# Second attention of a two-layer decoder trunk: both heads of a pair in one job for maxima and shifts, one score bank per head, weight sums on GpSimd alone

## The reference

```python
def mla_attention(h, w_in, q_norm, kv_norm, w_uq, w_ukv, w_o):
    ...                                   # q: 16 heads x (64 + 32), k: 64 + shared 32, v: 64
    def attend_block(args):               # one block of 128 queries, all 16 heads
        qn, qp, b = args
        q_pos = N_META + b * BLOCK + jnp.arange(BLOCK)
        s = (jnp.einsum('bqhd,bshd->bhqs', qn, k_nope)
             + jnp.einsum('bqhd,bsd->bhqs', qp, k_pe)).astype(jnp.float32)
        s = jnp.where(k_pos[None, :] <= q_pos[:, None], s, NEG_INF)
        p = jax.nn.softmax(s, axis=-1).astype(v.dtype)
        return jnp.einsum('bhqs,bshd->bqhd', p, v)
    ...
    return o @ w_o
```

## Time and profile before

| | |
|---|---|
| median of 3 executions | 3991.29 us (3990.94 to 4009.18) |
| profiled execution | 3988.05 us, of it 3986.3 us from the first to the last instruction |
| TensorE busy, whole span | 3469.2 us, 87% |
| VectorE, GpSimd, ScalarE busy | 2007.0, 1575.1, 1245.8 us |
| mean granted TensorE clock | 0.927 |
| second attention | about 1772 to 3024 us of the span |

### The profile page before, as it was taken

One profiled execution on the slowest core, in us unless ns is written; L12 is line 12 of the kernel. 1 busy time (PEld: TensorE's weight loads), 2 busy tenths in 40 slices (PEclk: granted clock), 3 DMA queues, 4 the chain that ended last, 5 costly groups with the idle time before them and its releaser, 6 DMA issues. The chain is left out here.

```text
span 3986.3 us, 60756 instructions
## 1 busy us (share of the span) xinstructions
PE 3469.2 (87%) x20523; PEld 2575.8 (65%) x20524; DVE 2007.0 (50%) x4183; ACT 1245.8 (31%) x2374; POOL 1575.1 (40%) x1257
## 2 busy tenths in 40 slices
PE   7999997996999959969999999999997996999920
PEld 5777775785888859955555555555554885888810
DVE  3555444674333336635666666666553653333306
ACT  3444444221222224432233233233223221222201
POOL 2222221343444315435665655655542223444302
PEclk8999998997999979977999999999898997999965
DMA  2101103554988849960101101101004447988519
GB/s 89 35 24 35 35 24 95 159 153 164 353 299 307 290 154 252 267 166 6 45 9 48 45 9 45 34 20 48 6 9 131 148 135 253 330 301 306 201 56 335
DMA packets 370814, 540.15 MB, mean 136 GB/s; under 512 B 94879, under 2 KB 291535, under 8 KB 363328
## 3 DMA queue, kind: packets, MB, share of 16 engines
q1 hardware_dynamic: 343584, 461.28, 37.0%
q0 software_dynamic: 27040, 76.40, 4.9%
HBM read 399.22 MB, written 146.96 MB: 137 GB/s over the span
## 5 line engine op out<-in xcount | busy, mean ns | idle before, releaser
L1965 POOL TENSOR_TENSOR ab_acc<-ab_acc,ab_pT 128x1024 f32<-128x1024 f32 (+4 forms) x208 | 424.4, 2040 | 491.4 <-ACT ab_pT L2009 486.7
L2009 ACT ACTIVATE ab_pT<-ab_S 128x1024 f32<-128x1024 f32 (+2 forms) x360 | 321.9, 894 | 864.3 <-PE ab_S L2110 536.5
L2021 DVE TENSOR_REDUCE ab_mx<-ab_W 128x1 f32<-128x400 f32 (+4 forms) x720 | 377.2, 560 | 374.8 <-PE ab_W L2124 207.4
L2167 PE MATMUL ab_O<-ab_pT,ab_v 128*64 128x512 f32 (+4 forms) x1408 | 353.7, 581 | 0.0
L2108 PE MATMUL ab_S<-ab_q_hi,ab_k_hi 97*128 97x512 f32 (+2 forms) x720 | 319.0, 443 | 0.9 <-DVE ab_q_hi L2038 0.9
L2124 PE MATMUL ab_W<-ab_k_hi,ab_q_hi 96*128 96x400 f32 (+4 forms) x720 | 246.9, 401 | 83.6 <-DMA ab_maskT<-in_mask_bT 28.5
L2108 PEld LDWEIGHTS ab_S<-ab_q_hi,ab_k_hi 97*128 97x128 f32 x720 | 142.1, 197 | 270.4 <-ACT ab_pT L2009 133.0
L1324 PE MATMUL ex_G<-ex_xT,ex_wg 128*128 128x160 f32 x2048 | 295.4, 303 | 5.2 <-DMA ex_wu<-in_moe_w_up 5.2
L1324 PEld LDWEIGHTS ex_G<-ex_xT,ex_wg 128*128 128x128 f32 x2048 | 284.6, 193 | 9.5 <-DMA ex_wu<-in_moe_w_up 6.0
L1324 PE MATMUL ex_U<-ex_xT,ex_wu 128*128 128x160 f32 x2048 | 288.6, 299 | 0.0
L1324 PEld LDWEIGHTS ex_U<-ex_xT,ex_wu 128*128 128x128 f32 x2048 | 281.6, 190 | 0.0
(11 more groups left out here) (297 smaller groups left out, 7195.9 us busy)
## 6 DMA issues: line engine op xcount, KB each, us to landing
ex_wg<-in_moe_w_gate SPq DMA_DIRECT2D x64, 1024.0 KB, 5.8
ex_wu<-in_moe_w_up SPq DMA_DIRECT2D x64, 1024.0 KB, 9.8
ex_wd<-in_moe_w_down SPq DMA_DIRECT2D x64, 1024.0 KB, 12.5
pr_o<-scratch_oT SPq DMA_DIRECT2D x34, 512.0 KB, 4.8
scratch_h<-pr_h SPq DMA_DIRECT2D x34, 512.0 KB, 4.9
scratch_xn<-pr_xn SPq DMA_DIRECT2D x34, 512.0 KB, 2.7
pb_y<-scratch_y SPq DMA_DIRECT2D x17, 1024.0 KB, 8.2
fi_y<-scratch_y SPq DMA_DIRECT2D x16, 1024.0 KB, 8.7
```

The lines of the kernel that those rows point to most:

```text
L1965: nc.gpsimd.tensor_tensor(to, to, pT[0:r, U % RING, :, 0:n], ALU.add).then_inc(added_pool, 1)
L2009: nc.scalar.activation(pT[0:r, U % RING, :, 0:n], S[0:r, U % 2, :, 0:n], ACT.Exp, scale=B_SCALE).then_inc(exped, 1)
L2021: nc.vector.reduce_max(mx[:, h, t, c:c + 1], W[:, j % 2, 0:n], AX.X).then_inc(emptied, 1)
L2167: last = nc.tensor.matmul(O[HD * h:HD * h + HD, G % 2, 512 - n:512], v[0:r, p % 2, h, b, :], pT[0:r, U % RING, h, 0:n], start=(U == opens[ ...
```

## The change

**Jobs of two heads.** `W` becomes four banks: two slots of two banks, one bank for each head. A scan or shift job now covers both heads, so there are half as many, and each is one instruction on VectorE over both banks (`W[:, j % 2, :, 0:n]`). On TensorE the two heads' scans come first and their two masks behind. The limits that fill `work[U]` are halved with the count.

**One score bank per head.** `S` becomes two banks. The scores of head h in unit U wait until the exponential of head h in unit U - 1 has read them (`exped`, counted per head now). ScalarE does one exponential per head instead of one over both: 720 instead of 360.

**Sums on GpSimd alone.** `on_dve`, `acc2` and the merging add are gone; GpSimd does all 352 sums.

**Six probability buffers** instead of four (`RING`), and a buffer `den0` of its own for tile 0. SyncE issues the four constants ahead of the first pair's loads instead of behind them.

The core of the diff:

```diff
-    RING = 4
+    RING = 6
-    def on_dve(U):
-        p, g, b = units[U]
-        return 0 < g < NG and b > 0 and (U - opens[p, g]) % 5 in (1, 3)
...
-        while taken < len(scans) and taken < (12 if U < 0 else min(2 * U + 44, 4 * U + 18)):
+        while taken < len(scans) and taken < (6 if U < 0 else min(U + 22, 2 * U + 9)):
...
-        S = s.ps("S", [P, 2, 2, 512])
+        S = s.ps("S", [P, 2, 512])
         O = s.ps("O", [P, 2, 512])
-        W = s.ps("W", [P, 2, 512])
+        W = s.ps("W", [P, 2, 2, 512])
...
-                load(0)
-                sp.dma_start(ident[:, :], io["ident"]).then_inc(consts, 16)
                 sp.dma_start(identb[:, :], io["identb"]).then_inc(consts, 16)
                 sp.dma_start(mask[:, :], io["mask_b"]).then_inc(consts, 16)
+                sp.dma_start(ident[:, :], io["ident"]).then_inc(consts, 16)
                 sp.dma_start(maskT[:, :], io["mask_bT"]).then_inc(consts, 16)
+                load(0)
...
-                    if U == closes[p, g]:
-                        if g > 0:
-                            pool.wait_ge(added_dve, dve_adds[U])
-                            nc.gpsimd.tensor_tensor(acc[:, G, :, :], acc[:, G, :, :], acc2[:, G, :, :], ALU.add).then_inc(merged, 1)
...
-                    nc.scalar.activation(pT[0:r, U % RING, :, 0:n], S[0:r, U % 2, :, 0:n], ACT.Exp, scale=B_SCALE).then_inc(exped, 1)
+                    for h in range(2):
+                        act.wait_ge(scored, 2 * U + h + 1)
+                        nc.scalar.activation(pT[0:r, U % RING, h, 0:n], S[0:r, h, 0:n], ACT.Exp, scale=B_SCALE).then_inc(exped, 1)
...
-                    nc.vector.reduce_max(mx[:, h, t, c:c + 1], W[:, j % 2, 0:n], AX.X).then_inc(emptied, 1)
+                    nc.vector.reduce_max(mx[:, :, t, c:c + 1].rearrange("p h a -> p (h a)"), W[:, j % 2, :, 0:n], AX.X).then_inc(emptied, 1)
...
-                    if 1 <= U <= NU and on_dve(U - 1):
-                        add(U - 1)
...
-                    if U >= 2:
-                        pe.wait_ge(exped, U - 1)
                     for h in range(2):
-                        to, qs = S[:, U % 2, h, 0:n], slice(at, at + n)
+                        to, qs = S[:, h, 0:n], slice(at, at + n)
+                        if U >= 1:
+                            pe.wait_ge(exped, 2 * U + h - 1)
...
-                    pe.wait_ge(merged, G + 1)
+                    pe.wait_ge(added, adds[closes[p, g]])
```

More of the change, by code:

```diff
@@ L1801, in attention_b @@
             for t in ([0] if g == 0 else []) + list(tiles_of(g)):
-                scans += [(p, g, h, t, c) for c in range(len(chunks_of(t))) for h in range(2)]
+                scans += [(p, g, t, c) for c in range(len(chunks_of(t)))]
     work = {U: [] for U in range(-1, NU + 8)}
@@ L1814, in attention_b @@
                 if g == 0:
-                    at.append(("shift", p, NG, 0))
-                at += [("shift", p, g, h) for h in range(2)]
+                    at.append(("shift", p, NG))
+                at.append(("shift", p, g))
                 assert U < 0 or U + 1 < opens[p, g]
@@ L1829, in attention_b @@
     pv_counts = [pv_count(U) for U in range(NU)]
-    dve_adds = [sum(1 for V in range(U + 1) if on_dve(V)) for U in range(NU)]
-    pool_adds = [sum(1 for V in range(U + 1) if units[V][1] < NG and not on_dve(V)) for U in range(NU)]
+    adds = pv_counts
     with ExitStack() as ctx:
@@ L1978, in _ @@
                     p, u = divmod(U, PU)
-                    if units[U][1] < NG and not on_dve(U):
+                    if units[U][1] < NG:
                         add(U)
@@ L2111, in score @@
                         if diagonal:
-                            last = nc.tensor.matmul(S[:, U % 2, h, 0:P], identb[:, :], maskT[:, :], start=False, stop=True)
-                    last.then_inc(scored, 1)
+                            last = nc.tensor.matmul(S[:, h, 0:P], identb[:, :], maskT[:, :], start=False, stop=True)
+                        last.then_inc(scored, 1)
                 def room(j):
@@ L2117, in room, with scan @@
                         pe.wait_ge(emptied, j - 1)
[L2119 removed]
+                def scan(j, p, g, t, c):
                     lo, n = chunks_of(t)[c]
@@ L2123, in scan, with shift @@
                     diagonal = c == len(chunks_of(t)) - 1
[L2124 to L2125 removed]
+                    for h in range(2):
+                        last = nc.tensor.matmul(W[:, j % 2, h, 0:n], q_hi[0:QD, p % 2, h, P * t:P * t + P], k_hi[0:QD, p % 2, h, lo:lo + n],
+                                                start=True, stop=not diagonal)
                     if diagonal:
                         d = min(P, n)
[L2128 removed]
+                        for h in range(2):
+                            last = nc.tensor.matmul(W[:, j % 2, h, n - d:n], identb[:, :], mask[:, 0:d], start=False, stop=True)
                     last.then_inc(filled, 1)
[L2131 removed]
+                def shift(j, p, g):
                     pe.wait_ge(m_ready, NG * p + g % NG + 1)
                     room(j)
[L2134 to L2136 removed]
+                    for h in range(2):
+                        for k in range(1 if g == NG else 4):
+                            one = m[:, h, 0:1] if g == NG else m[:, h, 4 * g + 1 + k:4 * g + 2 + k]
+                            last = nc.tensor.transpose(W[:, j % 2, h, P * k:P * k + P], one.to_broadcast([P, P]), ident[:, :])
                     last.then_inc(filled, 1)
@@ L2140, in divide @@
                     G = NG * p + g
-                    pe.wait_ge(merged, G + 1)
+                    pe.wait_ge(added, adds[closes[p, g]])
                     room(j)
                     for h in range(2):
-                        last = nc.tensor.matmul(W[HD * h:HD * h + HD, j % 2, :], ones[:, :], acc[:, G % 2, h, :], start=True, stop=True)
+                        last = nc.tensor.matmul(W[HD * h:HD * h + HD, j % 2, 0, :], ones[:, :], acc[:, G % 2, h, :], start=True, stop=True)
                     last.then_inc(filled, 1)
@@ L2153, in early @@
                         weights = pT[0:META, U % RING, h, 0:P]
-                        nc.tensor.matmul(W[HD * h:HD * h + HD, j % 2, 0:P], v[0:META, p % 2, h, 0, :], weights, start=True, stop=True)
-                        last = nc.tensor.matmul(W[HD * h:HD * h + HD, j % 2, P:2 * P], ones[0:META, :], weights, start=True, stop=True)
+                        nc.tensor.matmul(W[HD * h:HD * h + HD, j % 2, 0, 0:P], v[0:META, p % 2, h, 0, :], weights, start=True, stop=True)
+                        last = nc.tensor.matmul(W[HD * h:HD * h + HD, j % 2, 0, P:2 * P], ones[0:META, :], weights, start=True, stop=True)
                     last.then_inc(filled, 1)
```

70 lines of the change are left out of this document (18 added, 52 removed).

## The result

The changed kernel takes 3828.76 us, the median of four executions (3818.64 to 3833.54), against 3991.11 us for the kernel before beside it (3977.01 to 4009.18): ratio 0.9587, 95% interval 0.9544 to 0.9631. In the profiled executions it is 3818.64 us against 3988.05, 169 us less. The forecast was 84 us less. A later run of the same changed kernel gave 3831.64 us and a ratio of 0.9558 (0.9517 to 0.9599).

The account below looks back on a forecast made before the run. TensorE was taken to set the pace, stopped by waits on `W` for VectorE. Waits 65 us, merge 2.4, masks 5 and clock 12 sum to 84 us: 3904 us profiled, forecast 3907 us, range 3850 to 3969.

Parts of the forecast that it names:

- The rows of the waits: TensorE's five listed waits on `W` for VectorE: 73.6 us in 133 waits go, 20 us (10 to 35) stay.
- The uncounted part: Time lost at TensorE's waits on `W` beyond the listed waits: 23 us at most, nothing at least, 11 taken.
- half of seven such dips: Clock falls at the starts of pairs of heads, 3.4 us each; half of seven go, 12 us won (-20 to 60).
- Rival 1: TensorE gets full clock from the stage's start, where 61 us at half level cost 30: 3877 us; chance 0.12.
- Masks, constants, merge: In the stage: masks behind both scans win 5 us (0 to 14), constants first 0, the end merge's removal 2.4.
- The cover: GpSimd falls 3 us behind in group 3 and may fall 12 before the divide waits: no cost.
- the worked-out 899: GpSimd's busy time in the stage with all sums on it, 899 us, up from 712.
- Rival 3: GpSimd becomes the bound with full sums at 3.11 us, 159 us a pair against 153.5: 4004 us; chance 0.04.
- rival 2: ScalarE's two exponentials, 0.171 us longer per unit than one, hold TensorE: 62 us more, 3969 us; chance 0.06.
- Rivals 4 and 5: More of the stage at half clock: 250 us more gives 4032 us, 130 to 205 gives 3972 to 4010; 0.05 each.

Follow-up runs that it names:

- the split alone: The kernel before with only one score bank and one exponential per head changed: 4078.1 us, ratio 1.0188 (1.0146 to 1.0229).

## Why the prediction was right in sign and half in size

**What bounds, and what goes.** Right. TensorE set the pace, its stops were on `W`, and the room on `W` removed them: 160 of 170 us hang on it.

**The rows of the waits.** 78.6 less 15.1 is 63.5 us won; the forecast was 53.6, from five rows of 73.6 with 20 staying. Five us were missed because the small rows were left out of the sum, and five because 15 stay and not 20. Right within its bounds. What stays behind the shifts is 1.1 us a pair where 1.3 was worked out.

**The uncounted part: the first term that failed.** I put 11 us on it, half of 133 x 0.17, "because some of the spacing is there without a wait too". After, 95 to 103 us are won without the clock. Less 63.5 for the rows and 7 for the masks, 24 to 33 remain over the 126 stops that went, which is 0.19 to 0.26 us each. This is worked out as a remainder and not measured alone, but it holds in a single clean pair as well: 149.78 - 135.13 = 14.7, less 1.4 for the clock, 9.0 for rows (10.4 in 18 waits before, 1.4 in 2 after) and 0.9 for masks, leaves 3.4 over 16 stops, 0.2 each. So the whole of the 0.12 to 0.23 us by which a modelled end lies too late came back at each stop, and halving it was the error. That none of this spacing is there without a wait is an inference from the sizes; no run tests it.

**The clock: the step that failed most.** "I let half of seven such dips go: 12 us." It was about 53 to 62, of up to 75. Three things were missed. All dips went, not half. The long half-level stretches in pairs 4 and 7 were taken as chance, though the one in pair 4 begins right behind a stop of 1.19 us; together these pairs lost up to 27 us. And the half-level stretch at the stage's start ended at 1793 us instead of 1837, where I took it as given because TensorE was busy 55.9 of 61 us. That gave up to 21 us. The changed kernel's second run rose only near 1807 us, so a part of this is chance, but not all: in the ten traces of kernels with more room on `W` it rose between 1792 and 1810 us and stayed up through the first pair. In the two kernels with two banks for `W` and four for the scores it rose at 1837 and 1841. In the two with two banks for each it rose near 1810, but fell again to half for 31 us twice. Rival 1, which got 0.12, named the recovery at the start but not its size elsewhere. By the rule of the Trainium skill ("TensorE: Matmul & The Clock Gate", section "Why this matters for your kernels"), to keep TensorE busy without gaps, 63 us more had been worked out beside it, 3844 us in all. The measured time is 3828.76 us. The later pairs of the trace agree with it; the first, busy 158 of 166 us and at 0.92, does not fully. I weighed one row against the rule, the dense stretch at half clock, though such a stretch only shows that density does not lift the clock at once, not that stops do not lower it.

**Masks, constants, merge.** 7 us for 5, 0 for 0, 2.6 for 2.4: right.

**The sum.** Of the 169.4 us, rows are 63.5, the uncounted part 24 to 33, masks 7, the clock 53 to 62, the merge 2.6 and the earlier start, by chance, 4.3; the last 6 stay open.

**Sums on GpSimd.** The cover held: 855.0 us busy in the stage where 880 to 920 were expected. Of the 44 us under the worked-out 899, shorter low rests are 31. A later pair has 106.9 us of work in 135. ScalarE now waits for GpSimd to release a buffer 13 times, 12.8 us in all and 2.1 at most, where it never did before. No row of TensorE waits for it. Rival 3 is refuted.

**Exponentials.** 720 operations; TensorE doesn't wait for them in the changed kernel, so rival 2 is refuted there. That the split alone would cost 75 us I had not seen: I priced its edits one by one, and this price comes only from VectorE's sum behind it, which the same change takes away.

**Rivals 4 and 5** went the wrong way: the clock rose.
